# Decay factors of a chunked delta rule by way of memory instead of two matmuls, and the first transfer of x in two halves

## The reference, cut to what matters

```python
g = jnp.cumsum(g.reshape(B, H, N, C), axis=-1)
kb = k * beta[..., None]
decay = jnp.exp(jnp.where(incl, g[..., :, None] - g[..., None, :], NEG_INF))
L = jnp.where(strict, jnp.einsum('bhnid,bhnjd->bhnij', kb, k) * decay, 0.0)
T = lax.linalg.triangular_solve(L + eye, ..., left_side=True, lower=True)
u = jnp.einsum('bhnij,bhnje->bhnie', T, vb)
intra = jnp.where(incl, jnp.einsum('bhnid,bhnjd->bhnij', q, k) * decay, 0.0)
```

## Time and profile before

| | us |
|---|---|
| median of 3 runs | 1200.12 (1200.05 to 1201.42) |
| the profiled execution | 1200.0 |
| its span in the trace | 1198.2 |
| PE busy, share of the span | 1188.3, 99% |
| DVE, ACT, POOL busy | 753.2, 609.4, 110.8 |
| granted TensorE clock | 0.998 |

### The profile page before, as it was taken

The page is one execution under the profiler, slowest core; times in us unless marked ns, Lnnn a source line. Parts: engine busy times, 40 slices in busy tenths (PEclk is TensorE's granted clock), DMA queues, the critical chain, the costliest instruction groups (busy, mean ns, idle before and its releaser), DMA issues.

```text
span 1198.2 us, 16074 instructions
## 1 busy us (share of the span) xinstructions
PE 1188.3 (99%) x6330; PEld 992.3 (83%) x6330; DVE 753.2 (63%) x990; ACT 609.4 (51%) x895; POOL 110.8 (9%) x149
## 2 busy tenths in 40 slices
PE   9999999999999999999999999999999999999997
PEld 7899888888878888888888888888777778888886
DVE  5776977766575666556455554676665656676654
ACT  6656554644433456534434444574446446555443
POOL 0002020259700110000000000000000000000000
PEclk9999999999999999999999999999999999999999
DMA  8878776566744455555665686566556455454862
GB/s 290 259 207 249 207 198 192 165 207 182 205 135 139 143 163 149 179 187 171 207 192 188 193 293 197 184 199 221 202 187 217 158 193 176 126 156 151 297 195 96
DMA packets 145530, 229.24 MB, mean 191 GB/s; under 512 B 12658, under 2 KB 63538, under 8 KB 144432
## 3 DMA queue, kind: packets, MB, share of 16 engines
q1 hardware_dynamic: 142016, 214.59, 57.7%
q0 software_dynamic: 3120, 12.57, 3.3%
q10 hardware_dynamic: 320, 1.06, 0.2%
HBM read 220.35 MB, written 4.72 MB: 188 GB/s over the span
## 4 chain that ended last, share of the span: by engine, by line
PE 99%; DMA 0%; ACT 0%; DVE 0%; issue 0%; SPq 0%; POOLq 0%; POOL 0%; ACTq 0%
PE acc L2094 69%; PE acc L2084 10%; PE acc L2086 5%; PE aux L1973 4%; PE acc L2035 3%; PE aux L2283 1%; PE aux L2311 1%; PE acc L2425 1%; PE aux L2058 1%; PE aux L2172 1%; PE aux L2276 1%; PE aux L2304 1%; DMA raw_w<-in_w_in 0%; PE aux L2221 0%; PE aux L2213 0%; PE aux L2168 0%
## 5 line engine op out<-in xcount | busy, mean ns | idle before, releaser
L1406 DVE TENSOR_TENSOR lo_w<-raw_w,hi_w 128x1024 fp32r<-128x1024 f32 (+2 forms) x381 | 464.3, 1225 | 327.0 <-ACT hi_w L1002 325.3
L2094 PE MATMUL acc<-hi_w,h_both 128*128 128x512 f32 (+3 forms) x1800 | 559.5, 385 | 0.0
L1002 ACT ACTIVATE hi_w<-raw_w 128x1024 fp32r<-128x1024 f32 (+2 forms) x381 | 394.1, 1049 | 285.9 <-PE acc L2094 185.0
L2094 PEld LDWEIGHTS acc<-hi_w,h_both 128*128 128x128 f32 x1800 | 332.3, 188 | 67.6 <-issue 4.9
L2094 PE MATMUL acc<-lo_w,h_both 128*128 128x512 f32 (+3 forms) x900 | 341.1, 379 | 0.0
L2094 PEld LDWEIGHTS acc<-lo_w,h_both 128*128 128x128 f32 x900 | 169.4, 188 | 28.7
L2084 PE MATMUL acc<-h_both,hi_w 128*128 128x512 f32 x512 | 180.3, 397 | 0.0
L2086 PE MATMUL acc<-h_both,lo_w 128*128 128x256 f32 x512 | 142.9, 279 | 0.0
L2084 PEld LDWEIGHTS acc<-h_both,hi_w 128*128 128x128 f32 x512 | 96.1, 188 | 23.0
L2086 PEld LDWEIGHTS acc<-h_both,lo_w 128*128 128x128 f32 x512 | 96.4, 188 | 0.1
L2094 PE MATMUL acc<-hi_w,m_hi 128*128 128x512 f32 x224 | 87.7, 391 | 0.0
(11 more groups left out here) (355 smaller groups left out, 1177.8 us busy)
## 6 DMA issues: line engine op xcount, KB each, us to landing
raw_w<-in_w_in SPq DMA_DIRECT2D x275, 512.0 KB, 4.1
raw_w<-in_w_out SPq DMA_DIRECT2D x64, 512.0 KB, 4.7
raw_w<-in_w_branch_a SPq DMA_DIRECT2D x16, 512.0 KB, 4.6
raw_w<-in_w_branch_b SPq DMA_DIRECT2D x16, 512.0 KB, 4.8
raw_w<-in_cmp_k_w SPq DMA_DIRECT2D x8, 512.0 KB, 6.2
raw_w<-in_cmp_v_w SPq DMA_DIRECT2D x8, 512.0 KB, 6.2
raw_w<-in_w_in SPq DMA_DIRECT2D x8, 384.0 KB, 4.6
x_in<-in_x SPq DMA_DIRECT2D x8, 256.0 KB, 7.3
```

The costliest lines, as they stand in the source:

```text
L1002: act.activation(piece_flat(hi_w[slot], no), piece_flat(raw_w[no % RAW_SLOTS], no), ACT.Copy).then_inc(*hi_ready.event(no))
L1406: dve.tensor_tensor(piece_flat(lo_w[slot], no), piece_flat(raw_w[no % RAW_SLOTS], no), piece_flat(hi_w[slot], no).bitcast(F32), ALU.subtra ...
L2094: i = pe.matmul(to[:, t, 0:group.cols], x[at], w[:, k], start=first and k == 0 and m == 0, stop=last and k == n - 1 and m == 2)
```

## The change

Three things are done. First, the rows g_j no longer come from PE. POOL writes `gcum` to memory, transposed (`g_rows`: 128 partitions x 16 single numbers of 4 bytes), and reads it back onto all 128 partitions (`g_rows_back`: 1 MB into `g_row`). Their ticks: `g_rows` one after `v_shift` of h = 0, `g_rows_back` eight later. `gu` and the two matmuls of `gram` go, and with them `g_hi`, `g_lo` and `ones_r`. `decay` reads `g_row` and stands one tick earlier, no longer behind `gram`.

Second, the transposes of `tri_flip` and ACT's copies go. DVE makes the transposed matrix itself, since k·k is symmetric: bank 1 times `low_t` times the factors `k_low` along the row, two more operations of 128 x 512 at the end of `tri`. The row of factors comes through memory like g (`k_rows` with 2 x 512 numbers for each h, `k_rows_back` with 2 x 256 KB).

Third, the first 256 columns of x come as two transfers of 128 columns, each ahead of its half of weight piece 0, and PE transposes the second channel row after the first two products of the first.

```diff
+    at(conv_end("v", 0) + 2, "g_rows")
+    at(conv_end("v", 0) + 10, "g_rows_back")
...
+    for h, (away, back) in enumerate(((V_TICKS[0][-1] - 5, V_TICKS[0][-1] + 2), (2, 10))):
+        at(conv_end("v", h) + away, "k_rows", h)
+        at(conv_end("v", h) + back, "k_rows_back", h)
...
-            at(s, "gu", h, t)
             at(s + 1, "gram", h, t)
-            at(s + 2, "decay", h, t)
+            at(s + 1, "decay", h, t)
             at(s + 3, "tri", h, t)
-            at(s + 5, "tri_flip", h, t)
...
+                        sp.dma_start(x_in[:, :, cols], x[:, :, cols]).then_inc(
+                            *(x_ready[0].event(0) if k else x_half.event(0)))
                         sp.dma_start(piece_view(raw_w[0], 0)[:, k], piece_source(0)[:, k]).then_inc(
...
+            def g_rows():
+
+                pool.wait_ge(*dve_did.after("gcum"))
+                pool.dma_start(g_scratch.rearrange("n p -> p n"), gcum, allow_slow_non_contiguous=True).then_inc(
+                    *g_away.event(0))
+
+            def g_rows_back():
+                pool.wait_ge(*g_away.after(0))
+                pool.dma_start(g_row[:].rearrange("p t h c -> p (t h c)"),
+                               g_scratch.rearrange("n p -> (n p)").partition_broadcast(P)).then_inc(*g_back.event(0))
+
+            def k_rows(h):
...
+                for t in range(NT):
+                    pool.dma_start(k_scratch[rows[t]].rearrange("n p -> p n"), k_low[:, rows[t]],
+                                   allow_slow_non_contiguous=True).then_inc(*k_away[h].event(t))
+
+            def k_rows_back(h):
...
+                pool.wait_ge(*k_away[h].after(NT - 1))
+                pool.wait_ge(*dve_did.after("v_tap", 0, 6))
...
             def decay(h, t):
...
-                act.wait_ge(*pe_did.after("gram", h, t))
+                if h:
+                    act.wait_ge(*dve_did.after("tri", 0, t))
+                elif t == 0:
+                    act.wait_ge(*g_back.after(0))
+                    act.wait_ge(*dve_did.after("ssq", "k", 1))
...
             def tri(h, t):
                 c = chain[t]
                 dve.wait_ge(*act_did.after("decay", h, t))
+                dve.wait_ge(*pe_did.after("gram", h, t))
+                if h:
+                    dve.wait_ge(*blocks_out[0][t].after(3))
+                if t == 0:
+                    dve.wait_ge(*k_back[h].after(NT - 1))
...
+                link(dve.tensor_tensor(low_t[h][t][:], aux[:, 1].rearrange("p (i c) -> p i c", c=P), low_t[h][t][:],
+                                       ALU.mult))
+                dve.tensor_tensor(low_t[h][t][:], low_t[h][t][:], k_row[:, t, quad(h)],
+                                  ALU.mult).then_inc(*dve_did.event("tri_turned", h, t))
...
             def gram(h, t):
-                take(0, (act_did, "decay", h, t))
-                pe.wait_ge(*act_did.after("ones_r"))
-                take(1, (dve_did, "tri", h, t))
+                take(1, (dve_did, "tri_turned", h, t))
                 take(2, (dve_did, "tri", h, t))
-                pe.wait_ge(*dve_did.after("gu", h, t))
...
-                for m, part in enumerate((gu_hi[t], gu_lo[t])):
-                    pe.matmul(aux[:, 0], ones_r[:], part[:].rearrange("p i c -> p (i c)"), start=m == 0, stop=m == 1)
...
+                        if (row, m) == (0, 0):
+                            pe.wait_ge(*x_ready[0].after(0))
+                            x_row(1)
```

More of the change, by code:

```diff
@@ L533, in build @@
                   for i, n in enumerate(("low_m", "inv", "wide"))} for t in range(NT)]
-        gu_hi, gu_lo = ([arena(f"gu_{n}{t}", [P, QUAD, P], F32R, 48 + 8 * t + kb) for t in range(NT)]
-                        for n, kb in (("hi", 4), ("lo", 2)))
+        g_row = arena("g_row", [P, NT, HEADS, P], F32, 100)
+        k_row = arena("k_row", [P, NT, HEADS, P], F32, 64)
         low_t = [[arena(f"low_t{h}{t}", [P, QUAD, P], F32, (54 + 8 * t, 96 + 2 * t)[h]) for t in range(NT)]
@@ L611, in build @@
         raw_half = signal("raw_half", 16)
+        x_half = signal("x_half", 16)
         row_ready = signal("row_ready", 16)
@@ L636, in build @@
         v_shifted = {j: signal(f"v_shifted{j}", 16) for j in range(1, CONV)}
+        g_away, g_back = signal("g_away", 16), signal("g_back", 16)
+        k_away, k_back = ([signal(f"k_{n}{h}", 16) for h in range(2)] for n in ("away", "back"))
         solved_out = signal("solved_out", 16)
@@ L979, in _ @@
                      "solve": solve, "v_shift": v_shift, "inv_zero": inv_zero,
+                     "g_rows": g_rows, "g_rows_back": g_rows_back, "k_rows": k_rows, "k_rows_back": k_rows_back,
                      "norm1": norm1, "norm2": norm2, "y_last": y_last, "residual": residual, "att": att, "tail": tail_}
@@ L1044, in sq1 @@
                 t = n % 2
+                if n < 2:
+                    act.wait_ge(*x_half.after(0))
                 for m in range(n // 2 * 4, n // 2 * 4 + 4):
@@ L1083, in m_out @@
                     act.wait_ge(*dve_did.after("v_tap", 1, 6))
+                    act.wait_ge(*dve_did.after("tri", 1, 1))
                 act.activation(m_t[part][:, two(h, s)], pairs_of(c)[:, :, 1], ACT.Copy).then_inc(
@@ L1586, in lift @@
                 if (h, t) == (0, 0):
+                    dve.wait_ge(*dve_did.after("tri_turned", 1, 1))
                     dve.wait_ge(*blocks_back.after(3, NT - 1))
-                    for t_ in range(NT):
-                        dve.wait_ge(*act_did.after("tri_flip", 1, t_))
                 link(dve.tensor_tensor(inv_q, inv_q, over_heads(upto[:]), ALU.mult))
@@ L2130, in norm2_col_, with x_row @@
                 turn(aux[:, 0, 0:KT], norm2_rows[:]).then_inc(*pe_did.event("norm2_col"))
+            def x_row(k):
+                take(k % AUX, (dve_did, "x_lo", k))
+                for t in range(NT):
+                    last = turn(x_flipped(k)[:, t], x_in[:, t, k * P:(k + 1) * P])
+                last.then_inc(*pe_did.event("x_flip", k))
             def x_flip(n):
@@ L2134, in x_flip @@
                 for k in range(2 * n, 2 * n + 2):
-                    take(k % AUX, (dve_did, "x_lo", k))
-                    for t in range(NT):
-                        last = turn(x_flipped(k)[:, t], x_in[:, t, k * P:(k + 1) * P])
-                    last.then_inc(*pe_did.event("x_flip", k))
+                    x_row(k)
             def gcum_():
@@ L2173, in gram @@
                 last.then_inc(*pe_did.event("gram", h, t))
-            def tri_flip(h, t):
-                take(3, (act_did, "tri_flip", h, t))
-                pe.wait_ge(*dve_did.after("tri", h, t))
-                for i in range(QUAD):
-                    last = turn(aux[:, 3, i * P:(i + 1) * P], chain[t]["wide"][:, i])
-                last.then_inc(*pe_did.event("tri_flip", h, t))
             def pair_y(h, t):
@@ L2438, in _ @@
             turn(aux[:, 3, 0:KT], norm_rows[:]).then_inc(*pe_did.event("norm_col"))
-            x_flip(0)
+            pe.wait_ge(*x_half.after(0))
+            x_row(0)
             warm(2)
```

49 lines of the change are left out of this document (18 added, 31 removed).

## The result

The changed kernel took 1205.98 us (median of 5 runs, 1204.25 to 1208.1), the kernel before 1200.05 beside it: a ratio of 1.005, 95% interval 1.0039 to 1.0062. It is slower by 5.9 us, where 1196.6 was forecast. Its profiled execution took 1205.6 us, with a span of 1203.6 and a granted clock of 0.996. One execution of the kernel before, beside a later round, took 6818 us and is left out of the ratios.

A forecast was written before the change was run, and what follows sets the result against it. PE was taken to bound the kernel, holding 99% of the chain of waits. From 1200.1 us, 3.74 saved on PE and 0.2 lost at the start gave 1196.6 us, range 1195.6 to 1198.6.

The forecast's parts named there:

- What PE is relieved of: At the four grams and last four transposes: removed matmuls, transposes and one wait save 3.74 us of PE's queue.
- The price of a number: In g_rows' write: 0.032 us per number, 128 per DMA engine, so 4.2 us, below the slack; cost nothing.
- slack of 6.2: Weight load behind the first shifted copies: 1.5 us before ACT plus 4.6 behind, together 6.2 us, before PE waits.
- Rival 2: Saving partly given back: numbers cost 0.065 us each, 8.3 us, 2.1 over the slack, PE waits; 1198.7 us; chance 0.11.
- The one of h = 0 meets a calmer stretch: k_rows of h = 0, half of g_rows, was said to meet a calmer stretch of weight loads; cost nothing.
- PE needs it three pieces after: Split weight piece behind g_rows: PE needs it at 128.6 us, ready at 123.95, leaving 4.6 us.
- Rival 3: Slower: 0.203 us per number, g_rows lasts 26 us, PE stands 19.8 us; 1216.4 us; decides from 0.095; chance 0.09.
- The start: First products and first parts of x: 0.2 us lost, between 0.1 gained and 1.0 lost.
- Rival 1: Start loses 1.0 us instead of 0.2, by SP's added issue and smaller packets; 1197.4 us; chance 0.12.
- The decay steps: Gram, tri, lift and ACT's decay work: nothing late enough for PE to wait, 0.64 us left at gram(0, 1); cost nothing.
- If tri slipped by 1 us: At the grams waiting for bank 1: PE would then lose 0.4 us at each of three grams.
- The signs: Trace checks: loads land below 14 us, ACT's raw_w waits within 3 us, PE waits at start alone, q0 packets show number's price.

The follow-up runs named there:

- no_writes: no_front with the single numbers of g_rows and both k_rows replaced by whole rows of a constant (wrong values), reads kept; 1196.08 us, ratio 0.9967.
- no_g_write: no_front with only the 2048 single numbers of g_rows replaced by 16 whole rows of a constant; 1196.61 us, ratio 0.9976.
- no_k_write: no_front with only the numbers of k_rows replaced by whole rows of a constant; 1197.54 us, ratio 0.9983.
- apart: no_front with k_rows of h = 0 issued five ticks later, at tick 52, nothing left out; 1199.25 us, ratio 0.9995.
- no_front: The changed kernel with the old start: x in eight parts of 256 columns, four transposes ahead of the first product; 1204.74 us, ratio 1.0043.
- front_only: The kernel before with only the new start, the third part of the change; 1201.19 us, ratio 1.0008.
- turned: The changed kernel with old start, PE making gcum in rows and turning k_low, so whole rows are written; 1197.29 us, ratio 0.9977.
- act_warm: front_act with two more warm-up products, four instead of two; 1199.78 us, ratio 1.0000.
- front_act: front_only with the second transfer of 128 columns of x issued by ACT's queue instead of SP's; 1200.33 us, ratio 1.0005.

## Why the prediction was wrong, point by point

**What PE is relieved of** was right: 3.74 us forecast, 3.9 in the two traces. no_writes is 3.7 us below the 1199.79 beside it.

**The price of a number was mis-sized.** I took 0.032 us, the row nearest in size, from rows of 128 bytes. It was 0.073, between the two ends of the range (0.008 and 0.203). By the working itself 128 x 0.073 = 9.3 us is over the slack of 6.2, a stall of 3.1 us. Measured with `g_rows` alone it is 0.9 us of PE's waiting and 1.5 us in all; why it is less than 3.1 has no row. Rival 2, with 0.065 us, was near in the price, and its 1198.7 is 1.2 above what this write does alone. The packet shares of the 207 us stretch said what a packet of rows costs and nothing on single numbers. The guess that they are packed was right (64 to a packet), and the sign "the packets of q0 show the price of a number" was wrong: by their printed times they cost next to nothing. With 0.008 and 0.203 us as the two ends, rivals 2 and 3 deserved more than 0.20 together. The Trainium skill's rule (DMA: Bandwidth & Descriptors, Rules for kernel authors), one descriptor per element, agrees with the trace in kind; the estimate by its figure of 10.5 ns, which is per packet, was 21.5 us for `g_rows`, and measured was 9.3, with 64 numbers to a packet.

**"The one of h = 0 meets a calmer stretch" was the step that decided.** I read the tick in the list as a time. POOL's queue goes by its own waits: held by the numbers of `g_rows` until 128.0, it then issued 1 MB and the next 1024 numbers within 2 us, while the loads were still late. Without `g_rows` the numbers cost 0.5 us, without `k_rows` 1.5, and all together 8.7; with k_rows(0) 25 us later and nothing left out the kernel is 5.5 us faster. That is shown by no_g_write, no_k_write and apart, and no_writes shows that the 1 MB in between is not to blame.

**The slack was counted for one consumer only.** "PE needs it three pieces after" holds for the pieces. `conv_silu` stands behind the split on ACT, and `conv_back` on PE follows within one tick. That is where after stood for 5.2 us. In no_front, where the timing differs by a microsecond, the stall fell on `lo_w`; so the place is chance, the lateness is not.

**What a stall costs** was taken as its length. It costs more: after's 5.2 us were followed by eight transposes that took 1.59 us in place of 0.80, no_front's 3.7 us by 2.4 us at the 1.2 GHz level. No term of the sum had this.

**Rival 3** had the mechanism and the direction. Its price (0.203) and its stall (19.8 us) were too large, and its point of decision, 0.095 us per number for one write, was too high because it counted `g_rows` alone.

**The start** was forecast at 0.2 us lost and lost about 1.3 (1.2 by no_front, 1.4 by front_only). Rival 1 named one of its two causes, SP's added issue, and I set it aside with "the engines are full from 7 us on". They are, but between 3 and 6 us they are not, and the second part of x, issued 0.5 us later, came late. The other cause, the clock, was not thought of: the moved transposes were also PE's work ahead of the first product. The earlier landing of half of piece 0, by up to 0.4 us, brought nothing: its split starts at 5.41 us in after and in front_only, and at 5.41 in no_front and turned, which have the old start.

**The decay steps** came out nearly as forecast: no gram waits in after, `lift(0, 0)` ends at 337.02 and `pair_y` starts at 340.88, the table loads cost nothing. But the 0.64 us at gram(0, 1) were thin: with a late split ahead of `decay` it waits 0.9 to 1.0 us (no_front, apart). "If tri slipped by 1 us" was the right condition, and late loads meet it.

**The signs** did their work: ACT waited 7.79 us for `raw_w` (not over 3, it said), a load took 18.0 us to land (below 14), and PE waited for `lo_w` at 130 us and longest at `conv_back`, a place that the list of signs did not have.

**What stays open:** what tips the clock at the start in some executions and not in others. The work ahead of the first product is a likely part of it (act_warm, eleven executions), and not all, since the old start has it too. The slower pitch of turned, 0.7 us, is unexplained, and PE's remaining 0.3 us between 105 and 150 us in after have no row of their own. That the engines spend their time on each number of a packet is inferred from the landings; no row shows an engine at it.

## What to carry to other kernels

A transfer whose elements lie apart is priced by its numbers, not by its bytes, and it slows every other transfer while it runs; let TensorE turn so small a matrix, for 0.3 us, and send whole rows. Don't read its price off the printed times of its packets. When a cost is said to be covered by a lead, ask who else stands behind the waiting instruction on its engine, and whether the next such cost comes before the lead is won back. A queue without waits runs ahead of the list that orders it, so "later in the list" doesn't keep two transfers apart.

## What the runs showed of the hardware

- 2048 single numbers of 4 bytes, from 128 partitions to memory, took 9.3 us on the 16 DMA engines (0.073 us each per engine), in two ways measured. They stand in their queue as packets of 64 numbers whose printed times say nothing of that (45 packets, 1.5% of 16 engines, in 10 us). A 1 KB packet of a load beside them took 0.164 us instead of 0.050, and a 512 KB load issued at 110.2 us took 18.0 us to land.
- The column of the granted clock reads 1.00 in the first 10 us even where products take 0.43 to 0.50 us instead of 0.23 (after and front_act with the new start, no_writes with the old). There the pitch is the only sign of the lower level; after a stall in mid-kernel the column does show it (0.50).
- An issue of SP more, 0.5 us, within the first 3 us made the next transfer start 0.5 us later (3.13 against 2.64 us), and cost about 1.0 us at the end (1200.6, the quickest of front_only, against 1199.5 to 1199.8 of front_act).
